# RMS norms of a three-layer transformer kernel: eight chunks of squares added into two on VectorE, summed over partitions by two products instead of eight

## What is computed

```python
def rms_norm(x, g):
    xf = x.astype(jnp.float32)
    y = xf * lax.rsqrt(jnp.mean(xf * xf, axis=-1, keepdims=True) + RMS_EPS)
    return (y * g.astype(jnp.float32)).astype(x.dtype)

# one layer
mod = cond @ ada_w[i] + ada_b[i]
sh1, sc1, g1, sh2, sc2, g2 = jnp.split(mod, 6, axis=-1)
h = rms_norm(x, norm_mix[i]) * (1.0 + sc1) + sh1
x = x + g1 * mixer(h)
h = rms_norm(x, norm_ffn[i]) * (1.0 + sc2) + sh2
x = x + g2 * conv_ffn(h, ffn_w_up[i], ffn_conv_w[i], ffn_conv_b[i], ffn_w_down[i])
```

## Time and profile before

| | us |
|---|---|
| median of 3 runs | 1322.2 |
| lowest and highest run | 1312.95, 1325.44 |
| profiled execution | 1320.51 |
| its span | 1318.8 |
| TensorE busy | 1236.1 |
| VectorE busy | 533.2 |
| ScalarE busy | 247.9 |

### The profile page before, as it was taken

The page is one execution under the profiler, slowest core; times in us unless marked ns, Lnnn a source line. Parts: engine busy times, 40 slices in busy tenths (PEclk is TensorE's granted clock), DMA queues, the critical chain, the costliest instruction groups (busy, mean ns, idle before and its releaser), DMA issues.

```text
span 1318.8 us, 14278 instructions
## 1 busy us (share of the span) xinstructions
PE 1236.1 (94%) x5955; PEld 1074.2 (81%) x5955; DVE 533.2 (40%) x1006; ACT 247.9 (19%) x432; POOL 29.1 (2%) x84
## 2 busy tenths in 40 slices
PE   3899998999999998798989999998999989999997
PEld 3788887888888886687868888887888878888885
DVE  6345422645554416433255554444373322111123
ACT  2233302000000114345120000003333320000001
POOL 0000040000000000300000000000000000000000
PEclk8899888999999889899999999997999999999999
DMA  9866806967768600225098776862433034535420
GB/s 346 265 224 223 287 1 227 359 225 273 253 226 291 188 0 0 64 88 168 2 387 290 245 277 216 301 216 75 128 128 96 32 121 134 181 109 189 142 82 32
DMA packets 154865, 233.94 MB, mean 177 GB/s; under 512 B 9705, under 2 KB 127281, under 8 KB 154801
## 3 DMA queue, kind: packets, MB, share of 16 engines
q1 hardware_dynamic: 154801, 233.03, 51.3%
HBM read 231.93 MB, written 1.07 MB: 177 GB/s over the span
## 4 chain that ended last, share of the span: by engine, by line
PE 87%; DVE 6%; ACT 3%; DMA 2%; issue 1%; SPq 1%; DVEq 0%; ACTq 0%
PE PS L566 48%; PE PS L620 17%; PE PS L576 6%; PE PS L540 3%; PE PS L709 2%; PE PS L552 2%; DVE ada_acc L1318 1%; DMA slot<-in_ffn_w_up 1%; PE PS L884 1%; PE PS L694 1%; PE PS L821 1%; DMA ffn_work<-in_final_norm_g 1%; PE PS L818 1%; PE PS L958 1%; PE PS L717 1%
## 5 line engine op out<-in xcount | busy, mean ns | idle before, releaser
L566 PE MATMUL PS<-hT,slot 128*128 128x256 f32 x2992 | 672.2, 385 | 16.4 <-DMA slot<-in_ffn_w_up 8.7
L566 PEld LDWEIGHTS PS<-hT,slot 128*128 128x128 f32 x2992 | 578.5, 194 | 97.8 <-issue 14.0
L620 PE MATMUL PS<-act,slot 128*128 128x256 f32 x1056 | 238.9, 380 | 6.3 <-DVE act L1403 6.3
L620 PEld LDWEIGHTS PS<-act,slot 128*128 128x128 f32 x1056 | 200.7, 190 | 34.5 <-DVE act L1403 5.0
L1377 DVE TENSOR_SCALAR ffn_work<-PS,pcol 128x256 f32<-128x256 f32 x110 | 55.7, 540 | 381.7 <-PE PS L566 381.7
L1318 DVE SCALAR_TENSOR_TENSOR ada_acc<-ada_slot,cond,ada_acc 128x1024 f32<-128x1024 f32 x126 | 161.5, 1281 | 11.7 <-DMA ada_slot<-in_ada_w 2.9
L1084 ACT ACTIVATE ffn_work<-ffn_work 128x256 f32<-128x256 f32 x66 | 27.5, 417 | 642.9 <-DVE ffn_work L1387 642.9
L576 PE MATMUL PS<-oT,slot 128*128 128x256 f32 x384 | 86.5, 388 | 0.5 <-DVE oT L1578 0.5
L576 PEld LDWEIGHTS PS<-oT,slot 128*128 128x128 f32 x384 | 74.7, 195 | 11.2 <-DVE oT L1578 0.8
L540 PEld LDWEIGHTS PS<-ones,ada_acc 128*128 128x128 f32 x288 | 45.4, 250 | 4.6 <-DVE mod L1329 4.3
L1382 DVE SCALAR_TENSOR_TENSOR ffn_work<-PS,pcol,ffn_work 128x255 f32<-128x255 f32 x110 | 48.6, 475 | 0.8
(11 more groups left out here) (237 smaller groups left out, 744.7 us busy)
## 6 DMA issues: line engine op xcount, KB each, us to landing
ada_slot<-in_ada_w SPq DMA_DIRECT2D x144, 512.0 KB, 8.1
slot<-in_ffn_w_up SPq DMA_DIRECT2D x44, 1024.0 KB, 10.4
slot<-in_ffn_w_down SPq DMA_DIRECT2D x22, 1024.0 KB, 4.9
slot<-in_w_up SPq DMA_DIRECT2D x22, 1024.0 KB, 5.1
slot<-in_sb_w_in SPq DMA_DIRECT2D x12, 1024.0 KB, 7.2
slot<-in_w_in SPq DMA_DIRECT2D x11, 1024.0 KB, 5.4
slot<-in_w_down SPq DMA_DIRECT2D x11, 1024.0 KB, 4.9
slot<-in_dsa_w_in SPq DMA_DIRECT2D x10, 1024.0 KB, 5.4
```

Of the source, the lines that this page charges most:

```text
L566: last = mm(PS[:, bank, half * T:half * T + T], slot[s][:, k, m * P:(m + 1) * P], x[:, k, :], start=k == 0, stop=k == KC - 1)
L620: last = mm(PS[:, c // 2, (c % 2) * T:(c % 2) * T + T], w[:, j_odd * D + c * P:j_odd * D + (c + 1) * P], act[:, j_odd, :], start=start and ...
```

## The change

TensorE's `norm` no longer waits for parts of the squares. It waits once for `sq_summed` and multiplies `ones` with chunks 0 and 1 of `sq` only. VectorE gets a new function `sum_squares(parts)`: three `tensor_tensor` adds of two chunks each (128x512), in place into chunks 0 and 1, from chunks 2 and 3, 4 and 5, 6 and 7. Before the adds of a part it waits for that part's square (`sq_ready`), and from the second add on it waits for the add before (`sq_added`). The last add increments `sq_summed`. `sum_squares` is called at the start of VectorE's `norm`, ahead of `root()`; for the first norm it is called earlier, behind the copies to `pcol` and ahead of `ada(0, 0, ...)`. The slot is still handed back by the norm's first product.

```diff
@@ tensor engine, norm
                 fill(2)
-                for c in range(KC):
-                    if c in np.cumsum((0,) + parts):
-                        pe.wait_ge(sq_ready, bk("sq_ready").next())
-                    last = mm(PS[:, 4, 0:T], ones[:, :], sq[:, c, :], start=c == 0, stop=c == KC - 1)
+                pe.wait_ge(sq_summed, bk("sq_summed").next())
+                for c in range(2):
+                    last = mm(PS[:, 4, 0:T], ones[:, :], sq[:, c, :], start=c == 0, stop=c == 1)
                     if c == 0 and free_slot is not None:
                         last.then_inc(slot_used[free_slot], 1)
                 last.then_inc(unit_full[2], 1)
@@ vector engine
-            def norm(which):
-
+            def sum_squares(parts):
+
+                done = np.cumsum(parts)
+                for n in range(len(parts)):
+                    dve.wait_ge(sq_ready, bk("sq_ready").next())
+                    for c in range(max(2, done[n] - parts[n]), done[n], 2):
+                        if c > 2:
+                            dve.wait_ge(sq_added, bk("sq_added").value())
+                        ins = dve.tensor_tensor(sq[:, 0:2, :], sq[:, 0:2, :], sq[:, c:c + 2, :], ALU.add)
+                        if c < KC - 2:
+                            ins.then_inc(sq_added, 1)
+                            bk("sq_added").next()
+                ins.then_inc(sq_summed, 1)
+
+            def norm(which, parts):
+
+                if parts != FIRST:
+                    sum_squares(parts)
                 root()
@@ first norm
             ins.then_inc(unit_read[0], 1)
+            sum_squares(FIRST)
             ada(0, 0, range(KC))
             mods(0, 1, 1)
             mods(0, 0, 1)
-            norm(0)
+            norm(0, FIRST)
@@ the others: norm(1, AFTER_OUT) three times, norm(0, AFTER_FFN) twice, norm(None, AFTER_FFN)
```

More of the change, by code:

```diff
@@ L197, in build @@
         sq_ready = sem("sq_ready")
+        sq_added = sem("sq_added")
+        sq_summed = sem("sq_summed")
         x_part_ready = sem("x_part_ready")
@@ L1477, in _ @@
             out_projection(2)
-            norm(1)
+            norm(1, AFTER_OUT)
             mods(0, 5, 1)
@@ L1483, in _ @@
             mods(1, 0, 3)
-            norm(0)
+            norm(0, AFTER_FFN)
             mods(1, 3, 3)
@@ L1766, in _ @@
             out_projection(2, units=OUT_UNITS[2])
-            norm(1)
+            norm(1, AFTER_OUT)
             ffn(2)
-            norm(None)
+            norm(None, AFTER_FFN)
             for u in (2, 3):
```

## The result

| | before | changed |
|---|---|---|
| median, us (4 runs each) | 1321.8 | 1336.8 |
| lowest and highest | 1312.95, 1325.44 | 1334.81, 1339.44 |
| profiled execution, its span | 1320.5, 1318.8 | 1334.8, 1333.1 |
| TensorE busy | 1236.1 | 1227.0 |
| VectorE busy | 533.2 | 547.2 |

The ratio of the times is 1.0125, with a 95% interval of 1.007 to 1.0179: the change costs about 15 us, and by the interval 9 to 24. A second measurement gave 1338.7 against 1325.5, ratio 1.015 (1.0091 to 1.0208). The prediction was 1331 (1322 to 1341), slower by 9: the right side, within the range, and some 6 us short. 14 us of VectorE's busy time came, the 21 adds.

The account below looks back on a forecast made before the run. TensorE carries 87% of the chain, but around norms VectorE, the w_up transfer or TensorE comes last, varying by norm. Seven norm terms sum to +8.8 us on the 1322.2 median, giving 1331 us, range 1322 to 1341.

Parts of the forecast that it names:

- Item 1: First norm: the adds come between the pcol copies and the ada products, nothing covers the delay: +2.3 us.
- Items 2 and 3: AFTER_OUT norms of layers 0 and 1: product, SP's w_up load and the projection behind it come later: +3.4 us each.
- under the transfer: Clock may fall earlier and catch the four records (+0.7 us each) or mods before L566, covered by the w_up load.
- no position hides the adds: All three adds stand behind VectorE's earlier work in program order, so their 2.3 us is exposed wherever issued.
- Item 4: AFTER_FFN norm, layer 0: second mods begin 1.3 us earlier but take 1.7 longer at the lower clock: +0.4 us.
- Item 5: AFTER_FFN norm, layer 1: products finish 2.4 us earlier, mods take 9.8 and not 7.9: -0.5 us.
- Item 6: AFTER_OUT norm, layer 2: 3.4 us from the last xT for adds and products instead of 3.72: -0.4 us.
- Item 7: Final norm: Ln starts at 1306.97 and not 1306.78, behind adds and products: +0.2 us.
- 2.5 either way: Allowance over five starts of L566, each running at the lower clock about 1 us longer or shorter.
- the clock costs more: Rival: more work runs at 1.2 GHz in L566 starts, first mods and final transposes: +16, 1338 us; chance 0.17.
- TensorE's records are the bound: Rival: each record removed leaves the path, adds lie in VectorE's idle time: 18 us less, 1304 us; chance 0.04.

Follow-up runs that it names:

- 2: Kernel before plus VectorE's three adds per norm, their sums unused, all eight products kept: median 1326.2 against 1321.6 us, ratio 1.0012.
- 4: Changed kernel with slot 0 handed back by a one-column product of its own ahead of the wait for the adds: median 1329.1 us, ratio 1.0013 to the kernel before.
- 7: Changed kernel with adds issued where their squares are ready, in the AFTER_OUT and AFTER_FFN norms: median 1333.6 us, ratio 1.0108 to the kernel before.
- 9: Layer 0's AFTER_FFN norm alone in changed form on the kernel before: ratio 1.0036; changed kernel with only that norm as before: 1.0038; both against the kernel before.
- 3: Kernel before with six of each norm's eight products left out and no adds: median 1324.7 against 1321.6 us, ratio 0.9996.

## Why the prediction came out as it did

The direction and the two mechanisms with the largest terms were right, and the range held. That the time came within 6 us of 1331 is in part luck: a stage that the sum puts at nothing added 7.7, and two pieces that the change doesn't touch gave 5.5 back. By the steps of the sum:

- **Item 1, FIRST, +2.3:** measured +2.0. The adds took 2.14 and not 2.3; adds that wait for VectorE alone are linked closer than those that wait for two engines. Right, and confirmed by 2.
- **Items 2 and 3, slot norms, +3.4 each:** measured +4.1 each. The place is right (4). The failed term is the 0.62 from the product's start to SP's load: it belongs to a product at full clock. The row stands behind the output projection without a gap; the new product stands behind 3.3 us of idle time and needs 1.22. I had named this case, and priced it at 0.7 "under the transfer". It isn't under the transfer, because the transfer waits for that product. That no position hides the adds holds for the positions of the change alone: in 7 two of the three lie beside TensorE's slabs, and the product starts at 2.41 and not 3.22.
- **Item 4, +0.4:** counted from the first mods' end, 14.9 us and not 13.9: +1.1. The mods were 10.0, I had 9.8 (at 0.205 a record, where the earlier trace rows give 0.19 to 0.20; it was 0.209); the four records 2.04, I had 1.7. The first mods, which I left alone, ran 2.7 us shorter in the profiled executions of the changed kernel.
- **Item 5, -0.5:** +0.4, for the same two terms.
- **Item 6, -0.4:** -0.3.
- **Item 7, +0.2:** +1.2. Here the failed term is 1.03 for four records: 2.05, at the lower clock.

Counted as the prediction counts them, the norms sum to 2.0 + 4.1 + 4.1 + 1.1 + 0.4 - 0.3 + 1.2 = 12.6 and not 8.8. Most of the 3.8 between them is one mistake made in five places (the slot norms, AFTER_FFN and the end): the clock taken for work that now stands behind a wait was too high, or its price at the lower clock too low.

**The step that is missing** is the latent stage, +7.7. "L566 starts each time at 0.50 granted behind TensorE's idle time, and I let that stand", with "2.5 either way" over five starts, took the clock behind a norm for a scatter around a mean. It isn't small: the same stage gave 191.4 to 191.5 in four profiles with this norm changed, and 183.7 and 183.9 in the kernel before. By 9 it follows the mods and the norm ahead of it; some 3 of the 7.7 us go with the first mods' clock, which may be scatter after all, and the 4.4 that are left go with the norm's form. In the profiled execution the stick-breaking stage was 2.8 and the first mods 2.7 shorter, which offset part of it.

The rival "the clock costs more" (0.17, 1338 us) gave the time best, and half its mechanism. I had priced it at the starts, the first mods and the final transposes; it fell on the norm's own products, the second mods and above all on the latent stage. "TensorE: Matmul & The Clock Gate" of the Trainium skill, section "HAM oscillation — how this bites in real kernels", tells of short work between waits that keeps falling back. The q projections, 14.0 apart with a fall and 12.2 without, agree with it here. The rival "TensorE's records are the bound" was out, by 3. The rule of "VectorE: DVE Perf Modes" of the Trainium skill, section "The DRAIN you can't avoid", that a semaphore between Vector instructions costs nothing extra, was rightly set aside. Three linked adds took 2.14 to 2.28; three unlinked ones would take 1.9, an estimate from the earlier trace rows.

Three things stay open. How much of the latent stage's 7.7 us is the norm's form and how much the execution's. Why two, one or four of the q projections are hit, in other kernels one or two and two more in part: that is read from the traces, not explained. And most kernels' times lie in groups some us apart (the kernel before shows 1313, 1321, 1328 and 1331), which one profile each can't resolve.

## What to carry to other kernels

Before work is moved from the busiest engine to an idle one, find out what its first instruction releases: here the first of eight products handed back a weight slot, and making it wait for three adds cost 4 us twice, while the adds themselves cost nothing in the norms where nobody waited. If the sum must wait, hand the slot back with a tiny instruction of its own and issue each add where its operand is ready; this recovered the whole loss. Give TensorE work behind a wait the lower clock as one of its two prices, and look at the stages behind it too: work taken from TensorE's stream needn't show in the time at all.

## What the runs showed of the hardware

- Four records, a pair of 128x256 float32 products, took 2.04 us behind 3.3 us of idle time at 0.50 granted, 1.03 to 1.13 at full clock; the same four records behind the same wait took 1.10 in layer 2. 48 one-column records took 5.3 to 5.4 us at full clock and 10.0 to 10.2 at the lower one.
- A stage of 183.7 us, with the same instructions, took 181.4 to 191.5 us, with the granted clock at 0.95 and 0.90 on average. It repeated within 0.2 us in two profiles each of the kernel before and the changed kernel, the second time from a start 4.5 us later in the changed one. The stick-breaking stage, in three kernels that are the same program up to its end, took 170.2, 170.6 and 175.6, the last at 0.90 granted and the first at 0.94.
- Leaving out 84 of 5955 records of TensorE, with nothing in their place, left the time at a ratio of 0.9996 (0.9964 to 1.0028).
